# Order of work ahead of the first products, gatings by z over three attention steps, and a low part moved in POOL's queue

## What is computed

```python
h = rms_norm(x, norm_w)
proj = jnp.einsum('btd,de->bte', h, w_in) + b_in
(a_q, a_k, a_v, a_z, m_q, m_k, m_v, m_i, m_f, m_o, m_z, g_attn, g_mlstm) = jnp.split(proj, SPLIT_IDX, axis=-1)
attn = sliding_window_sink_attention(...)
branch_a = jnp.einsum('bte,ed->btd', attn * jax.nn.silu(a_z), w_branch_attn)
...
h_tilde = mlstm_chunkwise(mq, mk, mv, m_i, m_f)
h_m = sigmoid(m_o) * head_rms_norm(h_tilde, mlstm_norm_w) * silu(m_z)
branch_m = jnp.einsum('bte,ed->btd', h_m, w_branch_mlstm)
merged = sigmoid(g_attn) * branch_a + sigmoid(g_mlstm) * branch_m
return x + jnp.einsum('btd,de->bte', merged, w_out)
```

## Time and profile before

| | us |
|---|---|
| median of 3 runs | 1146.2 (1146.02 to 1146.5) |
| the profiled execution, whole | 1146.56 |
| its span | 1144.9 |
| PE busy | 1114.6 |
| DVE busy | 745.4 |
| POOL busy | 604.5 |
| ACT busy | 472.8 |

### The profile page before, as it was taken

The page is one execution under the profiler, slowest core; times in us unless marked ns, Lnnn a source line. Parts: engine busy times, 40 slices in busy tenths (PEclk is TensorE's granted clock), DMA queues, the critical chain, the costliest instruction groups (busy, mean ns, idle before and its releaser), DMA issues.

```text
span 1144.9 us, 16618 instructions
## 1 busy us (share of the span) xinstructions
PE 1114.6 (97%) x5419; PEld 888.5 (78%) x5419; DVE 745.4 (65%) x1205; ACT 472.8 (41%) x1125; POOL 604.5 (53%) x424
## 2 busy tenths in 40 slices
PE   5899999999999999999999999999999999999997
PEld 4688767767767768888888888888887888888886
DVE  4996887886786888566756675668678321645333
ACT  6355433543534535353635363546454212112311
POOL 6458546546455568656955685668542443531000
PEclk9999999999999999999999999999999999999999
DMA  6115114132132132112311232122209334432222
GB/s 210 52 46 133 38 57 119 38 108 67 37 110 74 36 110 67 38 38 83 96 43 38 74 93 54 37 73 86 63 7 367 126 93 148 155 115 73 92 74 92
DMA packets 110906, 99.06 MB, mean 87 GB/s; under 512 B 10324, under 2 KB 96464, under 8 KB 110848
## 3 DMA queue, kind: packets, MB, share of 16 engines
q1 hardware_dynamic: 97712, 68.96, 20.6%
q10 hardware_dynamic: 13136, 29.36, 7.8%
HBM read 76.22 MB, written 22.09 MB: 86 GB/s over the span
## 4 chain that ended last, share of the span: by engine, by line
PE 82%; DVE 9%; ACT 3%; DVEq 3%; issue 1%; ACTq 1%; DMA 1%; SPq 0%
PE ps L907 45%; PE ps L1140 15%; PE ps L1192 3%; PE ps L1187 3%; PE ps L1188 3%; PE ps L816 2%; PE ps L998 2%; PE ps L1114 1%; PE ps L1098 1%; PE ps L1047 1%; PE ps L1102 1%; PE ps L1111 1%; PE ps L1040 1%; DVE probs L1987 1%; DVE v L2199 1%
## 5 line engine op out<-in xcount | busy, mean ns | idle before, releaser
L727 POOL TENSOR_TENSOR ring_lo<-w,ring_hi 128x512 fp32r<-128x512 f32 x128 | 184.6, 1461 | 157.0 <-ACT ring_hi L1246 157.0
L907 PE MATMUL ps<-s_hi,ring_hi 128*128 128x512 f32 x512 | 203.9, 398 | 2.7 <-DVE ev L1882 2.7
L727 POOL TENSOR_TENSOR ring_lo<-t,ring_hi 128x512 fp32r<-128x512 f32 x96 | 135.9, 1421 | 127.2 <-ACT ring_hi L1246 127.2
L907 PE MATMUL ps<-s_lo,ring_hi 128*128 128x512 f32 x512 | 202.6, 396 | 0.0
L907 PE MATMUL ps<-s_hi,ring_lo 128*128 128x512 f32 x512 | 202.0, 395 | 0.0
L907 PE MATMUL ps<-h_hi,ring_lo 128*128 128x512 f32 x384 | 152.0, 396 | 0.0
L907 PE MATMUL ps<-h_hi,ring_hi 128*128 128x512 f32 x384 | 151.9, 396 | 0.0
L907 PE MATMUL ps<-h_lo,ring_hi 128*128 128x512 f32 x384 | 151.4, 394 | 0.0
L907 PEld LDWEIGHTS ps<-s_hi,ring_hi 128*128 128x128 f32 x512 | 96.2, 188 | 26.3 <-issue 7.2
L907 PEld LDWEIGHTS ps<-s_hi,ring_lo 128*128 128x128 f32 x512 | 96.2, 188 | 21.9 <-issue 2.6
L1246 ACT ACTIVATE ring_hi<-w 128x512 fp32r<-128x512 f32 x128 | 76.3, 621 | 86.1 <-PE ps L907 79.3
(11 more groups left out here) (300 smaller groups left out, 2214.1 us busy)
## 6 DMA issues: line engine op xcount, KB each, us to landing
w<-in_w_in SPq DMA_DIRECT2D x128, 256.0 KB, 2.9
xs<-in_x SPq DMA_DIRECT2D x8, 512.0 KB, 7.5
ga_scratch<-ev ACTq DMA_DIRECT2D x4, 1024.0 KB, 4.8
u_scratch<-silu_z ACTq DMA_DIRECT2D x8, 512.0 KB, 3.5
gm_scratch<-ev ACTq DMA_DIRECT2D x4, 1024.0 KB, 4.8
w_raw<-in_w_branch_attn SPq DMA_DIRECT2D x8, 512.0 KB, 3.7
u_a_f<-u_scratch SPq DMA_DIRECT2D x4, 1024.0 KB, 7.8
ev<-ga_scratch ACTq DMA_DIRECT2D x8, 512.0 KB, 3.4
```

The costliest lines, as they stand in the source:

```text
L727: return nc.gpsimd.tensor_tensor(flat(lo[:]), flat(raw_or_sum[:]), flat(hi[:]).bitcast(F32), ALU.subtract)
L907: mm = nc.tensor.matmul(ps[:, bank, :], w[:, k, :], h[:, k, :], start=(m == 0), stop=(m == PRODUCT - 1))
```

## The change

Four moves; nothing is added to or taken from what is computed.

```diff
@@ POOL @@
                 if later(i):
                     pool.wait_ge(w1_hi, i + 1)
                     low(w11, ring0).then_inc(w1_ready, 1)
-                pool.drain()
+                pool.wait_ge(w6_hi, i + 1)
+                low(t2, ring1).then_inc(w6_ready, 1)
                 pool.wait_ge(w21_in, 16 * i + 16)
                 add(t4[:], w21[:], t2[:], ALU.subtract).then_inc(sum_made, 1)
...
             def weights_of_pair(i):
-                pool.wait_ge(w6_hi, i + 1)
-                low(t2, ring1).then_inc(w6_ready, 1)
                 pool.wait_ge(w2_hi, i + 1)
@@ ACT @@
-            act.wait_ge(s324_made, 2)
-            A(s2[0][:], s2_f[:], ACT.Copy).then_inc(s_hi, 1)
             act.wait_ge(g_sum, 1)
             act.sem_inc(tile_out, 1)
...
             A(g_t1[0:8, :], g_t1[0:8, :], ACT.Ln, bias=1.0).then_inc(g_log, 1)
-            act.wait_ge(s324_made, 1)
+            act.wait_ge(s324_made, 2)
+            A(s2[0][:], s2_f[:], ACT.Copy).then_inc(s_hi, 1)
             A(s3[0][:], s3_f[:], ACT.Copy).then_inc(s_hi, 1)
...
-                    if n == 7:
+                    if n == 8:
                         act.wait_ge(u_half, g + 1)
@@ DVE @@
-            V.tensor_tensor(s3_f[:], f11[:], f21[:], ALU.subtract).then_inc(s324_made, 1)
-            V.tensor_tensor(s2_f[:], s1_f[:], f11[:], ALU.subtract).then_inc(s324_made, 1)
-            dve.drain()
...
             V.tensor_tensor(i_, i_, dense_ps(GATES)[64:72, :], ALU.add)
             V.tensor_tensor(f_, f_, dense_ps(GATES)[96:104, :], ALU.add).then_inc(g_sum, 1)
+            V.tensor_tensor(s3_f[:], f11[:], f21[:], ALU.subtract).then_inc(s324_made, 1)
+            V.tensor_tensor(s2_f[:], s1_f[:], f11[:], ALU.subtract).then_inc(s324_made, 1)
+            dve.drain()
...
-            low_part(s2, s2_f, 1)
             dve.drain()
             dve.wait_ge(g_log, 1)
...
             V.tensor_tensor_scan(b_, keeps, logf, 0.0, ALU.mult, ALU.add)
+            low_part(s2, s2_f, 1)
             low_part(s3, s3_f, 2)
...
-                    if n == 5:
-                        silu(2)
-                        silu(3)
+                    if n in (5, 6):
+                        silu(n - 3)
+                        dve.drain()
+                    if n == (6 if final(g, KV) else 7):
                         dve.wait_ge(attn_copied, EARLY * (g + 1))
                         V.tensor_tensor(silu_z[:, :, 0:EARLY * P], u_early[:], silu_z[:, :, 0:EARLY * P], ALU.mult)\
                             .then_inc(early_used, 1)
```

## The result

The changed kernel takes 1147.89 us (median of 20 runs, 1145.24 to 1150.07) against 1146.23 of the kernel before (20 runs beside them): ratio 1.0015, interval 1.0008 to 1.0022. A second series of 11 runs gave 1147.58, ratio 1.0012 (1.0003 to 1.0022). The forecast was 1142.0 with a range to 1144.6. Its profiled execution took 1149.55 us, 1.7 above the median; a second one, 1147.20, is shown beside it where they differ: in where PE's clock fell, and in step 3 of the attention also in one operation of DVE.

A forecast was written before the change was run, and what follows sets the result against it. PE was taken to bound the kernel, working 1114.6 of 1144.9 us, with gains only from about 8 us of waits. Terms 0.3 + 3.9 + 0 = 4.2 us off 1146.56 gave 1142.4, or 1142.0 for the median; range 1139.9 to 1144.6.

The forecast's parts named there:

- Step 1: Start, PE behind tile 2: gate sums put first remove the 4.2 us wait and 2.3 us of slow clock, 6.5 us.
- What is late next: Start, up to `turn_gates`: DVE's chain to the second v copy allows 1.5 us at most; the rest returns as new waits.
- rival (a): Start: DVE keeps POOL out through both scans, `turn_gates` starts at 93.4, gain 1.0, total 1141.3 us; chance 0.20.
- The start's net: Start, up to `turn_gates`: at 94.1 against 94.39 before, a gain of 0.3 us.
- Rival (b): Start: the clock falls in one of PE's new waits; at `turn_gates` 2.3 us are lost, total 1144.3 us; chance 0.18.
- Step 2: Attention steps 0 to 2: moved gatings end the waits for L1882 (2.7 us) and block 7's probabilities (1.2), gain 3.9 us.
- Step 2, step 3 of the attention: Last attention step: PE comes 1.05 us earlier but waits that longer for block 7; counted 0, between -1.2 and +1.0.
- Step 3: Pairs 1 to 31, POOL's queue: low part 2 comes up to 1.3 us later with 5.3 us of lead; counted 0, bound +1 us.
- Step 4: Attention, ACT's first-half store from n = 7 to n = 8: covered by the rest of the step, counted 0 us.
- Rival (d): Attention: block 6 is not earlier, combine(7) starts 0.8 us later than before, total 1151.8 us, slower; chance 0.05.

The follow-up runs named there:

- e_start: Kernel before with only the start's VectorE and ScalarE edits (gate sums ahead of the two token sums), GpSimd's queue unchanged: 1145.94 us, ratio 0.9998.
- e_sp0: Kernel before with the start as changed and product 6's low part ahead of t4 in pair 0 alone, attention as before: 1145.58 us, ratio 0.9993.
- e_attn: Kernel before with only the attention changed: silu(3) at n = 6, early gating at n = 7 (6 in the last step), half store at n = 8: 1147.79 us.
- e_gate7: Kernel before with the early gating alone moved to n = 7 (6 in the last step), store at n = 8: 1150.25 us, ratio 1.0035.
- e_silu6: Kernel before with silu(3) alone moved from n = 5 to n = 6, early gating left at n = 5: 1147.41 us, ratio 1.0011.
- e_silu8: Kernel before with silu(3) alone moved from n = 5 to n = 8, early gating left at n = 5: 1144.50 us, ratio 0.9986.
- e_after_p0: Changed kernel with product 6's low part moved ahead of t4 in pair 0 alone: 1147.24 us, ratio 1.0016 against the kernel before.
- e_best_s8: Kernel before plus changed start, product 6's low part moved in pair 0 alone, early v copies, early gating at n = 4, silu(3) at n = 8: 1139.73 us.

## Why the prediction was wrong, step by step

- **Step 1, the gates' PSUM place: right.** The wait of L816 went with its fall of the clock. "It fits by 0.2 us" held: no wait between tiles 3 and 4.
- **What is late next: right in kind and in sum, wrong in one wait.** `turn_gates` waited 2.63 (forecast 2.9), product 6 and product 2 waited 0.58 and 0.51 (1.9 and 0.9). POOL did not get between the scans: its row at 63.30 stands 6.20 us, through scan 2 and the first low part, nearly as in rival (a). But low part 6 was there at 79.4 by before's time, not at 82.0, and `turn_gates` at 92.2, 1.2 us before that rival's 93.4. The start's net, 0.3 forecast, measured 0.5 (`e_start`) and 0.7 (`e_sp0`), both within what a series can tell from nothing.
- **Rival (b), the fall of the clock: true and not exclusive.** It fell in both profiled executions of the changed kernel, where the forecast gave it 0.18, and in four of the six traces with that wait, so the chance was set too low. It comes on top of the other steps rather than in place of them.
- **Step 2, the attention's gatings: the step that failed.** 3.9 us gained were forecast, 1.3 lost were measured alone. The two waits that it priced did go in steps 0 to 2. "The wait for the probabilities of block 7 ... is then covered" came true there, but the step followed block 7 through combine(7) and normalise(7) and stopped; it put nothing at what comes behind. Behind them in DVE's queue stand select(7) and gate(6), and PE waits for gate(6) before the product of block 7: 1.71, 0.85 and 0.84 us in the changed kernel, 1.32, 1.48 and 1.48 in `e_attn`, which takes the whole gain back. The early gating was put ahead of both, and at a price of 2.03, not the 0.94 of its old place. The forecast had priced what leaves the front of L1882 and not who is queued behind the new place. combine(7), said to start at 167.8, started at 168.63.
- **Step 2, step 3 of the attention:** "between -1.2 and +1.0". `early_used` came at 412.7 in the first profile and 411.6 in the second (forecast 412.3), combine(7) at 414.5 and 413.4 (414.0), so the chain was read rightly; the wait behind it was 1.87 to 2.20, with up to 0.80 ahead of it at L1039, where the sum had 1.3: +0.6 and +3.0 in the two profiles, the larger one with DVE 1.2 us later and a fall of the clock.
- **Step 3, the low part in POOL's queue: failed.** 0 was forecast with a bound of 1; alone it costs 1.3, on top of the start 2.2, and in the changed kernel nothing that the runs can tell. The step asked only whether a product waits for POOL and found 5.3 us of lead. It left out that POOL's operations hold DVE's: the move took t4 out of a gap and lengthened the row that runs beside combine(4).
- **Step 4, ACT's store at n = 8: right, as far as the traces show.** ACT stands 6.0 to 6.1 us for `u_half` in steps 0 to 2 with the next pair's high parts behind it, and no wait of PE comes of it, as the step said. No run has the store alone.
- **Rival (d)**, 1151.8 on the slower side, was not what happened: block 6 was earlier, by 2.1 us at combine(6) (160.45 against 162.55). The right slower rival would have been a gating at n = 7 ahead of gate(6), which alone is the 1150.25 of `e_gate7`.

## What to carry to other kernels

When work moves back in an engine's queue, list what is queued behind its new place until the next operation that the bounding engine waits for, and price it at the duration that operations have there; `e_silu6` and `e_silu8` differ by two blocks of place and by 2.8 us. When work moves on an engine whose operations hold those of another, as POOL's hold DVE's here, look not only for who waits for its result but for gaps that it used to fill: here t4 cost nothing in a gap and 0.5 us per step behind it. And price each new wait of PE with its chance of a fallen clock.

## What the runs showed of the hardware

- **A wait of the same length lets the clock fall in one execution and not in another.** PE stood 2.6 us at `turn_gates` in six traces; the clock fell behind it in four (0.50 from 91.1 to 98 in the first profile of the changed kernel, from 94.6 to 98 in the second) and stayed at 1.00 in two. A wait of 2.19 us in step 3 was followed by 0.77 and 0.80, one of 2.20 in the same place of `e_attn` and of `e_after_p0` by 1.00; the first had another wait of 0.80 just ahead of it, `e_attn` one of 0.22. The Trainium skill says in "TensorE: Matmul & The Clock Gate", Part 1, of the slow matmuls at the start of a kernel that their number differs from run to run of one kernel. These rows show the same for waits in the midst of one.
- **A running operation of POOL held operations of DVE until it ended, and a row of DVE's held POOL.** The 128x4 operation at 133.87 took 1.16 us instead of 0.16, to the end of POOL's row. One product silu takes 0.64 us at n = 4 of the kernel before, where POOL is idle, and 1.78 at n = 5 and 1.13 at n = 8 of `e_best_s8`, beside POOL's rows. Not every small one is held: the 128x4 reciprocal at 129.86 of the kernel before took 0.18 us in the midst of POOL's row at 129.71. The other way, POOL's operation at 63.30 took 6.20 us where 1.28 is usual. It was issued 0.6 us ahead of DVE's scan 2, which ran its 2.25 us without delay, and so did the low part behind it; the second low part, from 68.27, took 3.37, and POOL ended at 69.50. The Trainium skill has for this, in "SBUF — State Buffer", section "Who interferes with whom", an exclusive lock on the port pair and the rule "Issue order, not op shape, decides who blocks." The row at 133.87 agrees with the lock, and the one at 397.32 fits the rule on the order; the row at 63.30 does not agree with that rule. DVE's scan in the same place:

```profile
63.91 2.25 DVE L1832 TENSOR_TENSOR_SCAN g_t<-ev,g_t 8x1024 f32<-8x1024 f32 x1
```
